# Gate-table products with the gate's high and low parts side by side as 256 fp32r columns, and the low half added to the staged table by VectorE

## The reference, cut to what matters

```
half_vals, half_idx = lax.top_k(scores, PEER_TOPK)
...
top_vals, top_pos = lax.top_k(cand_vals, PEER_TOPK)
expert_idx = jnp.take_along_axis(cand_idx, top_pos, axis=-1)
gates = jax.nn.softmax(top_vals, axis=-1)
...
    u = jnp.take(expert_u, i_t, axis=0)
    act = jax.nn.gelu(jnp.einsum('ted,td->te', u, x_t)) * g_t
    return jnp.einsum('te,ted->td', act, jnp.take(expert_v, i_t, axis=0))
```

## Time and profile before

| | |
|---|---|
| median of 3 runs | 3994.22 us (3994.01 to 3995.06) |
| profiled execution | 3999.43 us, of which the span 3997.5 us |
| mean granted TensorE clock | 0.992 of full speed |
| PE busy | 3923.6 us, 98% |
| DVE busy | 2696.9 us, 67% |
| ACT / POOL busy | 1453.8 us / 1305.6 us |

### The profile page before, as it was taken

How to read it: one execution, slowest core, us unless ns; L and a number is a source line. 1 busy time by engine, 2 the same in 40 slices (tenths; PEclk the granted TensorE clock), 3 DMA queues, 4 the chain that set the end, 5 groups by cost and what they waited for, 6 DMA issues and landing times.

```text
span 3997.5 us, 57499 instructions
## 1 busy us (share of the span) xinstructions
PE 3923.6 (98%) x18154; PEld 3235.6 (81%) x18154; DVE 2696.9 (67%) x4417; ACT 1453.8 (36%) x1925; POOL 1305.6 (33%) x887
## 2 busy tenths in 40 slices
PE   8999999999999999999999999999999999999997
PEld 5777888888888878888767778888888888788886
DVE  6753649967774278778577546498777732888785
ACT  5433333333333333333444333333333333333334
POOL 1100003433331077666101000044333401767651
PEclk9999999999999999999999999999999999999999
DMA  3222223445454599999212223234445446999992
GB/s 112 74 84 90 100 86 129 147 161 187 173 184 147 192 338 367 353 350 346 106 68 75 89 90 106 80 137 145 172 176 189 169 147 206 348 371 357 353 332 74
DMA packets 323761, 740.32 MB, mean 185 GB/s; under 512 B 30496, under 2 KB 161696, under 8 KB 319904
## 3 DMA queue, kind: packets, MB, share of 16 engines
q1 hardware_dynamic: 104400, 381.73, 26.8%
q10 hardware_dynamic: 174160, 222.40, 16.5%
q0 software_dynamic: 45056, 134.38, 9.0%
HBM read 618.87 MB, written 119.54 MB: 185 GB/s over the span
## 4 chain that ended last, share of the span: by engine, by line
PE 94%; issue 2%; DVE 2%; ACT 1%; POOL 1%; DMA 0%; ACTq 0%; DVEq 0%; POOLq 0%; SPq 0%
PE bank L1180 61%; PE bank L1395 24%; PE bank L1375 4%; PE bank L1242 1%; PE bank L1232 1%; PE bank L1250 1%; ACT hi L439 0%; PE bank L1325 0%; PE bank L1324 0%; PE bank L1227 0%; PE bank L1323 0%; DVE xl L776 0%; DMA vrow<-in_stream,tail_v 0%; ACTq L645 0%; DVE lo L764 0%
## 5 line engine op out<-in xcount | busy, mean ns | idle before, releaser
L1180 PE MATMUL bank<-xh,hi 128*128 128x512 f32 x3264 | 1308.7, 401 | 24.4 <-DVE xl L776 18.7
L1180 PE MATMUL bank<-xh,lo 128*128 128x512 f32 x3264 | 1275.8, 391 | 0.0
L1180 PE MATMUL bank<-xl,hi 128*128 128x512 f32 x3264 | 1275.5, 391 | 0.0
L764 DVE TENSOR_TENSOR lo<-raw,hi 128x1024 fp32r<-128x1024 f32 (+1 forms) x532 | 645.3, 1213 | 520.3 <-ACT hi L439 485.7
L439 ACT ACTIVATE hi<-raw 128x1024 fp32r<-128x1024 f32 x724 | 739.7, 1042 | 318.9 <-DMA raw<-in_stream 188.0
L386 POOL TENSOR_TENSOR lo<-raw,hi 128x1024 fp32r<-128x1024 f32 x192 | 480.7, 2504 | 975.7 <-ACT hi L439 975.5
L1180 PEld LDWEIGHTS bank<-xh,hi 128*128 128x128 f32 x3264 | 616.2, 189 | 161.8 <-DVE xl L776 23.8
L1180 PEld LDWEIGHTS bank<-xh,lo 128*128 128x128 f32 x3264 | 614.8, 188 | 130.2
L1180 PEld LDWEIGHTS bank<-xl,hi 128*128 128x128 f32 x3264 | 616.7, 189 | 123.9 <-issue 5.6
L398 POOL DMA_INDIRECT hval<-early,tail_h x256 | 383.7, 1499 | 427.9 <-DMA early<-eo 347.2
L1395 PE MATMUL bank<-hi,ah 128*128 128x512 f32 x1536 | 476.0, 391 | 11.3 <-DVE al L1081 9.8
(11 more groups left out here) (209 smaller groups left out, 3512.1 us busy)
## 6 DMA issues: line engine op xcount, KB each, us to landing
raw<-in_stream SPq DMA_DIRECT2D x724, 512.0 KB
early<-eo ACTq DMA_DIRECT2D x256, 256.0 KB, 2.1
gate_table<-stage ACTq DMA_DIRECT2D x24, 2048.0 KB, 7.4
gb<-gate_table ACTq DMA_DIRECT2D x64, 768.0 KB
eb<-early ACTq DMA_DIRECT2D x64, 768.0 KB
hval<-early,tail_h POOLq DMA_INDIRECT x256
vrow<-in_stream,tail_v POOLq DMA_INDIRECT x256
hT<-in_xT ACTq DMA_DIRECT2D x2, 1024.0 KB, 8.3
```

Source lines behind the costliest of these rows:

```text
L764: dve.tensor_tensor(lo[k % RING][:, 0:w], raw[k % RAW][:, 0:w], hi[k % RING][:, 0:w].bitcast(f32), ALU.subtract).then_inc(lo_split, 1)
L1180: ins = pe.matmul(out_ap, st[slot][:, a:a + P], mv, start=first and i == 0, stop=last and i == 2)
```

## The change

The gate is split like the weights: ScalarE rounds all gates to fp32r once per layer (`gates_h`), and VectorE subtracts that from the gates' row of `tabs`, which so becomes the low part. LB and RB become fp32r, and LB holds for each token 128 columns of the high part and then 128 of the low part, so that one fp32r matmul of 256 moving columns gives both halves of the token's table. A quad now fills two banks (6 and 7, or 0 and 1, in turn). ScalarE copies the high halves into `stage` in two pieces; VectorE then adds the low halves in place, in two pieces, and signals `hot_added`, for which TensorE (before it writes those banks again) and the DMA of the table wait.

VectorE builds a quad by four `tensor_tensor` operations of 128 x 512 in place of one and four `tensor_scalar`: the comparison with the first keys, that with the second, and two products with the low and the high gates, with two waits of VectorE for itself in between (`link`). The add of quad n - 2 is ordered behind the one-hots of quad n.

The hot stage is spread over 64 experts (36 to 99) instead of 48, with two quads in even and one in odd ones (`quads_at`). GpSimd splits up to e = 123 instead of 99, and the exponents come at e = 110. The hot stage of VectorE and ScalarE is written out, where it was a loop.

```diff
-HOT_E, POOL_E, LOOP_E, LAST_T = 36, 100, 100, 116
+HOT_E, POOL_E, LAST_T = 36, 124, 116
+EXP_TAIL = 110
...
-HOT_END = HOT_E + 4 * NTB
-HALF_Q = QUADS // 2
-DVE_LAYER, DVE_PAIR, DVE_TURN = 203, 12, 2
+HOT_END = HOT_E + QUADS * 2 // 3
+HOT_PARTS = ((HOT_E, (EARLY * EG - HOT_E) // 8), (EARLY * EG, (HOT_END - EARLY * EG) // 8))
+def quads_at(e):
+    k = (e - HOT_E) % 8
+    first = (e - HOT_E) // 8 * 12 + k // 2 * 3 + k % 2 * 2
+    return range(first, first + 2 - k % 2)
+DVE_LAYER, DVE_PAIR, DVE_TURN = 396, 12, 2
...
-    LB = sb("LB", o_r + 24 * KB, [P, 2, 4, NK])
-    RB = sb("RB", o_r + 28 * KB, [P, 2, 4, NK])
+    LB = sb("LB", o_r + 16 * KB, [P, 2, 4, 2, NK], f32r)
+    RB = sb("RB", o_r + 24 * KB, [P, 2, 4, NK], f32r)
+    gates_h = sb("gates_h", o_t + 36 * KB + 512, [P, M], f32r)
+        hot_bank = [bank[6:8], bank[0:2]]
...
                 exponents(c)
     act.wait_ge(tabs_ready, (l + 1) * MT)
-    apart(act)
-    for part, row in enumerate((even(HOT_E), odd(EARLY * EG))):
-        with act.Fori(0, NTB // 4) as i:
-            for b in range(2):
-                act.wait_ge(table_out[b], l * (NTB * 8) + i * 16 + (part * NTB * 4 + 16))
-                for z in range(4):
-                    for q in range(2):
-                        n = part * HALF_Q + b * 8 + z * 2 + q
-                        act.wait_ge(hot_used, 2 + l * QUADS + i * 16 + n + 1)
-                        act.activation(stage[b][:, :, (z * 2 + q) * 4:(z * 2 + q) * 4 + 4],
-                                       bank[6 + q][:, :].rearrange("p (t k) -> p k t", k=NK), ACT.Copy)\
-                           .then_inc(staged, 1)
-                    e = b * 4 + z
-                    dense_gelu(N_U + HOT_E + part * 2 * NTB + e, i * 16 + (row + even(e)), i)
-                act.wait_ge(staged, 2 + l * QUADS + i * 16 + (part * HALF_Q + b * 8 + 8))
-                act.dma_start(gate_table[bass.ds(i * 2 + (part * NTB // 2 + b), 1), :, :]
-                              .rearrange("a p n -> (a p) n"),
-                              stage[b][:, :, :].rearrange("p k t -> p (k t)")).then_inc(table_out[b], 16)
-
-    for e in range(HOT_END, LOOP_E):
+    act.activation(gates_h[:, :], tabs[:, 2, :], ACT.Copy).then_inc(gates_hi, 1)
+    for e in range(HOT_E, HOT_END):
+        for n in quads_at(e):
+            t, q = n // DC, n % DC
+            if q == 0:
+                act.wait_ge(table_out[t % 2], l * (NTB * 8) + (t // 2 * 16 + 16))
+            act.wait_ge(hot_used, 2 + l * QUADS + (n + 1))
+            for z in range(2):
+                out = act.activation(stage[t % 2][:, :, q * 4 + z * 2:q * 4 + z * 2 + 2],
+                                     hot_bank[n % 2][z][:, :].rearrange("p (t h k) -> p h k t", h=2, k=NK)[:, 0], ACT.Copy)
+            out.then_inc(staged, 1)
+        dense_gelu(N_U + e, even(e) if e < EARLY * EG else odd(e))
+        for n in quads_at(e):
+            t, q = n // DC, n % DC
+            if q == DC - 1:
+                act.wait_ge(hot_added, 2 + l * QUADS + (n + 1))
+                act.dma_start(gate_table[t:t + 1, :, :].rearrange("a p n -> (a p) n"),
+                              stage[t % 2][:, :, :].rearrange("p k t -> p (k t)")).then_inc(table_out[t % 2], 16)
+
+    for e in range(HOT_END, LAST_T):
         dense_gelu(N_U + e, odd(e))
-        if e == LOOP_E - 4:
+        if e == EXP_TAIL:
             exponents(NBLK - 1)
-    with act.Fori(0, (LAST_T - LOOP_E) // 8) as i:
-        for e in range(8):
-            dense_gelu(N_U + LOOP_E + e, i * 16 + odd(LOOP_E + e), i)
...
-    dve.wait_ge(tabs_ready, (l + 1) * MT)
-    apart(dve)
-    with dve.Fori(0, QUADS // 2) as i:
-        for u in range(2):
-            dve.wait_ge(hot_used, l * QUADS + i * 2 + u + 1)
-            dve.tensor_tensor(RB[:, u, :, :], iota[:, :].unsqueeze(1).to_broadcast([P, 4, NK]),
-                              tabs[:, 1, bass.ds(i * 8 + u * 4, 4)].unsqueeze(2).to_broadcast([P, 4, NK]),
-                              ALU.is_equal)
-            for q in range(4):
-                t = i * 8 + u * 4 + q
-                last = dve.tensor_scalar(LB[:, u, q, :], iota[:, :], tabs[:, 0, bass.ds(t, 1)],
-                                         tabs[:, 2, bass.ds(t, 1)], ALU.is_equal, ALU.mult)
-            last.then_inc(hot_ready, 1)
+    dve.wait_ge(gates_hi, l + 1)
+    link(dve.tensor_tensor(tabs[:, 2, :], tabs[:, 2, :], gates_h[:, :].bitcast(f32), ALU.subtract))
+
+    def one_hots(n):
+
+        u, four = n % 2, [P, 4, NK]
+
+        def column(table):
+            return table[:, n * 4:n * 4 + 4].unsqueeze(2).to_broadcast(four)
+
+        def tokens():
+            return iota[:, :].unsqueeze(1).to_broadcast(four)
+
+        found = LB[:, u, :, 0, :].bitcast(f32)
+        dve.wait_ge(hot_used, l * QUADS + (n + 1))
+        eq = dve.tensor_tensor(LB[:, u, :, 0, :], tokens(), column(tabs[:, 0, :]), ALU.is_equal)
+        link(eq)
+        dve.tensor_tensor(RB[:, u, :, :], tokens(), column(tabs[:, 1, :]), ALU.is_equal)
+        link(dve.tensor_tensor(LB[:, u, :, 1, :], found, column(tabs[:, 2, :]), ALU.mult))
+        dve.tensor_tensor(LB[:, u, :, 0, :], found, column(gates_h[:, :].bitcast(f32)), ALU.mult).then_inc(hot_ready, 1)
+
+    def add_low(n):
+
+        t, q = n // DC, n % DC
+        dve.wait_ge(staged, l * QUADS + (n + 1))
+        for z in range(2):
+            cells = stage[t % 2][:, :, q * 4 + z * 2:q * 4 + z * 2 + 2]
+            add = dve.tensor_tensor(cells, cells,
+                                    hot_bank[n % 2][z][:, :].rearrange("p (t h k) -> p h k t", h=2, k=NK)[:, 1], ALU.add)
+        add.then_inc(hot_added, 1)
+
+    for n in range(QUADS):
+        one_hots(n)
+        if n >= 2:
+            add_low(n - 2)
+    add_low(QUADS - 2)
+    add_low(QUADS - 1)
...
-    with dve.Fori(0, (LAST_T - POOL_E) // 8) as i:
-        for k in range(8):
-            split(l, N_U + POOL_E + k, i)
-    for e in range(LAST_T, NK + AHEAD):
+    for e in range(POOL_E, NK + AHEAD):
...
         e += n
     experts(e, HOT_E - e)
-    for part in range(2):
-        with pe.Fori(0, NTB // 4) as i:
+    for at, turns in HOT_PARTS:
+        with pe.Fori(0, turns) as i:
             for k in range(8):
-                e = HOT_E + part * 2 * NTB + k
+                e = at + k
                 pe.wait_ge(act_evac, l * A_ALL + A_U + i * 8 + e + 1)
                 pe.wait_ge(lo_split, RAW + l * T + i * 8 + N_U + e + 1)
+                quads = quads_at(e)
                 for c in range(DC):
-                    if c % 4 == 0:
-                        u = c // 4
-                        n = l * QUADS + i * 16 + (part * HALF_Q + k * 2 + u)
-                        pe.wait_ge(hot_ready, n + 1)
-                        pe.wait_ge(staged, n + 1)
+                    if c % 4 == 0 and c // 4 < len(quads):
+                        n = quads[c // 4]
+                        pe.wait_ge(hot_ready, l * QUADS + i * 12 + n + 1)
+                        pe.wait_ge(hot_added, l * QUADS + i * 12 + n + 1)
                         for q in range(4):
-                            ins = pe.matmul(bank[6 + u][:, q * P:(q + 1) * P], RB[:, u, q, :], LB[:, u, q, :],
-                                            start=True, stop=True)
+                            ins = pe.matmul(hot_bank[n % 2][q // 2][:, q % 2 * 2 * NK:(q % 2 + 1) * 2 * NK],
+                                            RB[:, n % 2, q, :], LB[:, n % 2, q, :, :].rearrange("p h k -> p (h k)"),
+                                            start=True, stop=True, skip_group_check=True)
                         ins.then_inc(hot_used, 1)
                     ins = three(bank[4 + k % 2][:, :], ((N_U + e) % RING, c * P), xh[:, c, :], xl[:, c, :],
                                 c == 0, c == DC - 1)
```

More of the change, by code:

```diff
@@ L83 @@
 QUADS = M // 4
-HOT_END = HOT_E + 4 * NTB
-HALF_Q = QUADS // 2
-assert TB // 4 == DC and HOT_E + 2 * NTB == EARLY * EG and HOT_END < LOOP_E
-DVE_LAYER, DVE_PAIR, DVE_TURN = 203, 12, 2
+HOT_END = HOT_E + QUADS * 2 // 3
+HOT_PARTS = ((HOT_E, (EARLY * EG - HOT_E) // 8), (EARLY * EG, (HOT_END - EARLY * EG) // 8))
+assert TB // 4 == DC and HOT_END < EXP_TAIL < LAST_T and (POOL_E - AHEAD) % 8 == 0
+def quads_at(e):
[3 more added lines that the diff above has]
+DVE_LAYER, DVE_PAIR, DVE_TURN = 396, 12, 2
 LOWEST = -3.0e38
@@ L281, in trunk_kernel @@
         top_ready, ex_ready, slots_ready, turned, tabs_ready = sem("top_ready"), sem("ex_ready"), sem("slots_ready"), sem("turned"), sem("tabs_ready")
-        hot_ready = sem("hot_ready")
+        hot_ready, hot_added, gates_hi = sem("hot_ready"), sem("hot_added"), sem("gates_hi")
         hot_used = sem("hot_used")
@@ L427, in _ @@
             act.sem_inc(act_evac, 2)
-            act.sem_inc(staged, 2)
             for u in range(2):
@@ L756, in _ @@
             dve.sem_inc(gate_scaled, 2)
+            dve.sem_inc(hot_added, 2)
             dve.sem_inc(ple_scaled, 2)
```

## The result

The changed kernel takes 4015.68 us (median of 4 runs, 4013.35 to 4019.67), the kernel before on the same chip 3994.11 us (4 runs, 3990.69 to 3995.06). The ratio is 1.0053, 95% interval 1.0042 to 1.0065: **slower by 0.5%**, 21.6 us. The profiled execution of after has a span of 4012.1 us, 14.6 more than the profiled one of before (3997.5); the latter was some 5 us over its median. Outside the two changed stages the profiled executions of all kernels here take 3120 to 3127 us, that of before the most, so the medians are the better measure.

The account below looks back on a forecast made before the run. TensorE bounds the kernel before; with the change, VectorE with GpSimd's lock bounds the hot stage and eats TensorE's 80 us gain. At +3.4 us per layer, 3994 + 7 = 4001 us; 8-in-10 range 3945 to 4050.

Parts of the forecast that it names:

- the likeliest of three: Whole kernel against before, within 8 us counted as same: slower 0.42, same 0.30, faster 0.28.
- The mechanism: Hot stage: VectorE with GpSimd becomes the bound and eats TensorE's gain; +3.4 us per layer, +7 in all.
- TensorE's saving: Hot-stage quads fall from 0.907 to 0.49 us, two experts take 12.35 us; 80 us gained if nothing else binds.
- VectorE's load: Hot stage: a quad costs VectorE 3.31 us, three take 9.93 us of TensorE's 12.35 per two experts.
- The lock: Hot stage: GpSimd's splits and VectorE's one-hots exclude each other, not the adds; 2.17 and 1.53 us per two experts.
- the walk: Event-by-event hot-stage period of 13.63 us, 436.2 us per layer against 435.2; variations 433 to 445, middle 438.7.
- the rival of the bad order: VectorE's hot-stage queue: splits never meet the adds, period 14.4 us, 4046 in all; chance with slow adds 0.17.
- TensorE's waits: At the quad matmuls TensorE idles some 40 us per layer, ended by VectorE's high-gate product or its add.
- the one-hots' mean: VectorE's one-hot operations in the hot stage: means near 0.9 us rather than 0.685.
- What lies beside other work: ScalarE's copies, gate rounding and subtraction (under 1 us each), last `select`, exponents and later splits: all cost nothing.
- The clock: Hot stage: TensorE's gaps of 1.3 us every 13.6 are counted as no clock loss.
- What was to cost nothing elsewhere: Around and behind expert 99: last `select` about 50 us, exponents at e = 110, splits for 100 to 123 delay nothing.

Follow-up runs that it names:

- e1: Changed kernel with ScalarE's rounding of the gates moved from behind expert 35 to behind expert 33: 4001.93 us, ratio 1.0018 to the kernel before.
- e2: Changed kernel with GpSimd's splits of tiles 36 to 99 cut to 16 of 1024 columns, the rest not computed: 3932.93 us, ratio 0.9844 to before.
- e3: Changed kernel with early gate rounding, and VectorE instead of GpSimd making the low parts of tiles 36 to 99: 3916.78 us, ratio 0.9806 to before.
- e5: Changed kernel with early gate rounding, and the adds of quad n - 2 ahead of quad n's one-hots: 4028.06 us, ratio 1.0085 to before.
- e6: Kernel before, without the change, but VectorE instead of GpSimd making the low parts for experts 36 to 83: 3994.01 us, ratio 1.0001.
- e4: Changed kernel with early gate rounding, and VectorE's operations in each quad reordered to cover its two waits for itself: 3958.64 us, ratio 0.9908 to before.

## Why the prediction was right, and which step failed

**In sum.** Forecast 4001, slower the likeliest of three; measured 4015.7. The mechanism was right, and a second one was missing. Without the missing one (e1) the kernel takes 4001.93 us, the point that was forecast, and is 6.3 us over before, less than the 8 us that I had called no change. So the sum was right for the mechanism that it held, but that the likeliest of the three came true is luck: a term of 14 us that I hadn't seen made the kernel clearly slower.

**TensorE's saving: right.** The quad at 896.06 takes 0.47 us to the next start; 12.38 us per two experts (e2, e3) against 12.35. The whole gain of 80 us was there to be had: e3 got 79.

**VectorE's load: right.** In the period above the two held operations lose 2.20 and 1.55 us; 13.731 less these is 9.98, forecast 9.93. The adds take 417 ns as the earlier trace rows had them, and their stride costs nothing.

**The lock: right in kind and size.** Walked 2.17 and 1.53, measured 2.20 and 1.55; forecast period 13.63, measured 13.731; forecast +3.4 us per layer, +3.5 in e1. That the last two agree within 0.1 is luck: the walk itself gave +1.0, and the 3.4 was the middle of its variations. e2 shows that it is GpSimd's splits that eat the gain in the periods; e5 shows that the rival of the bad order was real too, only not the order that the kernel has. The Trainium skill's rule ("SBUF — State Buffer", section "SBUF: two separate sides") is that whichever starts first, a GpSimd operation or one of VectorE with two SBUF inputs, holds the shared ports for its whole instruction. These rows agree: an operation of 0.69 us takes 2.89 beside a split, and the adds, which read one input from a bank, take 0.74 a pair inside one.

**TensorE's waits: where forecast, by the add.** 67.0 us in both layers, 33.5 per layer where I had said 40. The records understate it: a wait is counted from a matmul's modelled end, 0.16 us behind the time at which the next could have started, and the quad behind a wait takes 0.55 instead of 0.47 (890.04 to 890.59). With 0.24 more in each of 32 periods it is 41.

**A slip.** I wrote that the one-hots' mean would be near 0.9 us. My own sum of 3.70 us lost in twelve operations gives 0.69 + 0.31 = 1.0; measured are 0.99 (the mean of the four groups above).

**The step that failed** is in "What lies beside other work": "The rounding of the gates and the subtraction (under 1 us each) lie between the last `tabs` and the first quad, for which VectorE was ready well before TensorE came." The durations were looked at, the queue was not. VectorE was ready, at 791.5, but the rounding is written behind the loop that ends with expert 35, and ScalarE does its queue in order. It began at 808.72, when TensorE had been ready for the first quad since 807.09, and everything behind it became a chain on the path: 0.51 us, then 2.38 instead of 0.55 by the same lock that I had costed for the one-hots only, then four one-hots. The stage is 7.3 us longer by it; e1 takes 13.8 us away in both layers by moving that one instruction. My walk took the tables as ready when the stage began; it went through the period and not through the first quad.

**The clock: right for the periods, wrong for the start.** Gaps of 1.1 us every 13.7 left the clock at 1.00 in the hot stretch. The gap of 7.3 us, which I had not foreseen, was followed by 0.76 of full clock over 5 us, as the earlier trace rows had it behind 4.78 us.

**What was to cost nothing elsewhere: right.** The last `select`, the exponents at e = 110 and the splits from 100 on left the 152.3 us behind expert 99 as they were.

## What to carry to other kernels

Where VectorE's operations are held beside GpSimd's, as here those with two SBUF inputs and the small `tensor_scalar`, the two engines have one budget between them: their times must be added, not laid side by side. And moving a GpSimd operation of 2.4 us to a VectorE that is already nearly full (1.2 us there) can be the whole gain. An edit that shortens the bound engine by 80 us is worth what the next engine leaves over, so walk through one period with all queues. And walk through the first turn too: a small preparing instruction costs what its place in its queue makes it wait, not what it takes.

## What the runs showed of the hardware

- An operation of VectorE that comes up just behind the start of a split of 2.4 us loses 2.08 to 2.20 us to it (e5, after), and one that stands behind two adds from a bank 1.55 us (after).
- `tensor_scalar` of 128 x 128 from SBUF, which has one tensor input, is held as well: 335 ns in the median of before, up to 2547 beside a split; the mean fell from 603 to 352 without splits (e6).
- fp32r products of 256 columns hold 0.12 us from start to start also when each has a stationary side of its own that VectorE wrote just before: 0.47 us for four.
- The place of two operations of 0.335 us, with the same work on every engine, moved the kernel by 26 us (e1 against e5), and the place of these and a comparison, which also covers VectorE's waits for itself, by 43 (e1 against e4).
